# The last layer's x rows are stored while tokens are chosen, and the experts' weighed results are added onto them in the output

## The reference

```
def expert_choice_moe(h, w_router, w_gate, w_up, w_down):
    aff = softmax(h @ w_router)                        # 16 experts
    g, idx = lax.top_k(swapaxes(aff, 1, 2), cap)       # each expert takes its cap = 128 best tokens
    xs = h[idx]
    hid = silu(xs @ w_gate[e]) * (xs @ w_up[e])        # 1024 -> 512
    y = (hid @ w_down[e]) * g[..., None]               # 512 -> 1024
    return zeros((n, d)).at[idx.reshape(-1)].add(y.reshape(-1, d))

for l in range(2):
    ...
    x = x + g2 * expert_choice_moe(modulate_2(x, sh2, sc2), w_router[l], w_gate[l], w_up[l], w_down[l])
return x
```

## Time and profile before

| | us |
|---|---|
| median of 3 runs | 4846.79 (4844.91 to 4851.37) |
| span of the profiled execution | 4847.7 |
| choosing, from the first row copy to the experts' first instruction | 4444.9 to 4483.3 |
| experts of the last layer, to the start of the last stage | 4483.3 to 4821.2 |
| last stage, `add_store` | 4821.2 to 4847.7 |

### The profile page before, as it was taken

How to read it: one execution, slowest core, us unless ns; L and a number is a source line. 1 busy time by engine, 2 the same in 40 slices (tenths; PEclk the granted TensorE clock), 3 DMA queues, 4 the chain that set the end, 5 groups by cost and what they waited for, 6 DMA issues and landing times. The chain is left out here.

```text
span 4847.7 us, 89240 instructions
## 1 busy us (share of the span) xinstructions
PE 4373.6 (90%) x39266; PEld 3433.8 (71%) x39266; DVE 2090.7 (43%) x3010; ACT 1367.4 (28%) x2034; POOL 1059.3 (22%) x756
## 2 busy tenths in 40 slices
PE   6998996999998989999989889997999788996997
PEld 3878885999894468888867657764776574774775
DVE  2027545444444233323422244426665414434886
ACT  2114213222221110000012133324665212322774
POOL 2310123444432123333322010021221211010211
PEclk9999997999999999999999899998999888998998
DMA  7310100000007311111131000037997210002998
GB/s 279 100 49 7 49 23 27 4 4 4 4 4 293 109 35 49 51 48 48 48 108 32 29 20 1 18 126 276 304 301 235 84 33 23 1 27 109 345 375 287
DMA packets 322593, 480.30 MB, mean 99 GB/s; under 512 B 43665, under 2 KB 201322, under 8 KB 313042
## 3 DMA queue, kind: packets, MB, share of 16 engines
q1 hardware_dynamic: 301778, 399.61, 24.0%
q0 software_dynamic: 17024, 63.11, 4.6%
q10 hardware_dynamic: 3456, 12.58, 0.7%
HBM read 420.71 MB, written 54.53 MB: 98 GB/s over the span
## 5 line engine op out<-in xcount | busy, mean ns | idle before, releaser
L3919 DVE TENSOR_TENSOR l_experts_lo<-l_raw_room,l_experts_hi 128x1024 fp32r<-128x1024 f32 x256 | 300.0, 1219 | 59.0 <-ACT l_experts_hi L3852 58.5
L3852 ACT ACTIVATE l_experts_hi<-l_raw_room 128x1024 fp32r<-128x1024 f32 x256 | 256.0, 1058 | 63.8 <-PEq L3458 28.6
L185 PE MATMUL mlp_ps<-h_hi,mlp_w_hi 128*128 128x512 f32 x512 | 200.8, 392 | 9.1 <-DVE h_lo L595 9.1
L185 PE MATMUL mlp_ps<-h_lo,mlp_w_hi 128*128 128x512 f32 x512 | 199.9, 391 | 0.0
L185 PE MATMUL mlp_ps<-h_hi,mlp_w_lo 128*128 128x512 f32 x512 | 199.9, 390 | 0.0
L1812 POOL TENSOR_TENSOR rec_lv<-rec_ab,rec_masks 128x512 f32<-128x512 f32 x120 | 145.2, 1227 | 246.2 <-DVE rec_ab L1729 159.4
L1748 DVE TENSOR_TENSOR rec_x<-rec_x,rec_all_ps 128x1024 f32<-128x1024 f32 (+1 forms) x100 | 111.4, 1114 | 196.8 <-PE rec_all_ps L1530 196.8
L2393 ACT ACTIVATE mlp_hid_hi<-mlp_pos 128x1024 f32 x32 | 34.0, 1062 | 569.3 <-DVE mlp_pos L2403 569.3
L160 POOL CAST mlp_w_hi<-mlp_w 128x1024 fp32r<-128x1024 f32 x64 | 66.8, 1043 | 497.2 <-issue 228.0
L185 PE MATMUL mlp_ps<-mlp_hid_hi,mlp_w_hi 128*128 128x512 f32 x448 | 174.3, 389 | 0.0
L185 PE MATMUL mlp_ps<-mlp_hid_lo,mlp_w_hi 128*128 128x512 f32 x448 | 174.3, 389 | 0.0
(11 more groups left out here) (717 smaller groups left out, 11457.8 us busy)
## 6 DMA issues: line engine op xcount, KB each, us to landing
l_raw_room<-in_w_gate_dram SPq DMA_DIRECT2D x128, 512.0 KB, 6.7
l_raw_room<-in_w_up_dram SPq DMA_DIRECT2D x128, 512.0 KB, 8.0
l_experts_raw_down<-in_w_down_dram SPq DMA_DIRECT2D x64, 1024.0 KB, 8.8
rec_out_w_ada<-in_w_ada_dram SPq DMA_DIRECT2D x24, 1024.0 KB, 12.1
mlp_w<-in_w_mlp_up_dram SPq DMA_DIRECT2D x32, 512.0 KB, 3.9
mlp_w<-in_w_mlp_down_dram SPq DMA_DIRECT2D x32, 512.0 KB, 3.8
l_choose_w_ada<-in_w_ada_dram POOLq DMA_DIRECT2D x16, 1024.0 KB, 16.5
l_in_w<-in_w_in_dram SPq DMA_DIRECT2D x18, 512.0 KB, 3.9
```

Of the source, the lines that this page charges most:

```text
L185: mm = self.nc.tensor.matmul(ps[0:rows, c, 0:n], w[b][:, k, 0:rows], x[:, k, t0:t0 + n], start=(k + j == 0), stop=(k == kt - 1 and j == 2))
L3852: nc.scalar.activation(hi[:, q % RING], piece(e, u), ACT.Copy).then_inc(hi_done, 1)
L3919: nc.vector.tensor_tensor(lo[:, q % RING], piece(e, u), hi[:, q % RING].bitcast(F32), ALU.subtract).then_inc(lo_done, 1)
```

## The change

The last layer alone is changed; the layer before it keeps `acc_dram`, the zeroing and ACT's `outputs`. In the last layer:

- `choose_tokens` turns, copies and stores 16 row tiles instead of 8: after `hT`'s 8 to `h_dram` come x's 8 from `xT` to the output, through the same two buffers. PE then spreads the gate into `pT`, and ACT copies it to `gate_row`. Nothing is zeroed, and `acc_dram` isn't written.
- `run_experts` has DVE weigh `pY` by `gain` and `gate_row` in one instruction of 128x1024 (`gated_outputs`), between the low parts of the units 3 and 4, and ACT's `outputs` isn't called. POOL's indirect adds go to the output.
- `add_store` is gone.

```diff
-def add_store(nc, name, ident, xT, acc, gate, out):
...
@@ choose_tokens
+        jobs = [(hT, h_dram, t) for t in range(rows)]
+        if final is not None:
+            xT, x_dram, gate, gate_row = final
+            jobs += [(xT, x_dram, t) for t in range(rows)]
...
-                sp.wait_ge(zero_set, 1)
-                for t in range(rows):
-                    sp.dma_start(acc_dram[t * P:(t + 1) * P, :], zero[:]).then_inc(zero_stored, 16)
+                if final is None:
+                    sp.wait_ge(zero_set, 1)
+                    for t in range(rows):
+                        sp.dma_start(acc_dram[t * P:(t + 1) * P, :], zero[:]).then_inc(zero_stored, 16)
                 load_ahead(sp)
-                for t in range(rows):
-                    sp.wait_ge(row_copied, t + 1)
-                    sp.dma_start(h_dram[t * P:(t + 1) * P, :], out[:, t % 2]).then_inc(row_stored[t % 2], 16)
+                for i, (_, dram, t) in enumerate(jobs):
+                    sp.wait_ge(row_copied, i + 1)
+                    sp.dma_start(dram[t * P:(t + 1) * P, :], out[:, i % 2]).then_inc(row_stored[i % 2], 16)
...
-                        tr = nc.tensor.transpose(ps[:, t % 2, k], hT[:, k, t * P:(t + 1) * P], ident)
+                        tr = nc.tensor.transpose(ps[:, i % 2, k], src[:, k, t * P:(t + 1) * P], ident)
                     tr.then_inc(row_turned, 1)
...
+                if final is not None:
+                    pe.wait_ge(aff_copied, 1)
+                    for k in range(KT):
+                        mm = nc.tensor.matmul(pT[:, k * P:(k + 1) * P], gate[:, k:k + 1].to_broadcast([P, P]), ident,
+                                              start=True, stop=True)
+                    mm.then_inc(gate_spread, 1)
                 pe.wait_ge(chosen, 1)
...
+                if final is not None:
+                    act.wait_ge(gate_spread, 1)
+                    nc.scalar.activation(gate_row, pT[:, 0:D], ACT.Copy)
@@ run_experts
-                    if step >= 2:
+                    if step >= 2 and gate_row is None:
                         outputs(step - 2)
...
+                def gated_outputs(e):
+                    dve.wait_ge(used, place[e, UNITS - 1] + 1)
+                    if e >= 2:
+                        dve.wait_ge(added[e % 2], 16 * NG * (e // 2))
+                    nc.vector.scalar_tensor_tensor(ys[:, e % 2], pY[:].rearrange("p c t -> p (c t)"), gain[:, 0, e:e + 1],
+                                                   gate_row, ALU.mult, ALU.mult).then_inc(y_read, 1)
...
-                for step in range(E_N + 1):
+                for step in range(E_N + 2):
                     if step < E_N:
-                        for u in range(1 if step else 4, UP):
+                        for u in range(1 if step else 4, 4):
+                            low(step, u)
+                    if step >= 2 and gate_row is not None:
+                        gated_outputs(step - 2)
+                    if step < E_N:
+                        for u in range(4, UP):
                             low(step, u)
@@ second_layer
-                    scratch["acc"][0:tokens, :], raw, a["w_down_2"][layer])
+                    out if last else scratch["acc"][0:tokens, :], raw, a["w_down_2"][layer], gate_row)
```

More of the change, by code:

```diff
@@ L3413, in choose_tokens @@
 def choose_tokens(nc, name, ones, ident, norm_groups, w_router, groups, idx, gain, quarter_idx, h_dram, acc_dram,
-                  load_ahead, beside=None):
+                  load_ahead, beside=None, final=None):
     hT = norm_groups[0][3]
@@ L3438, in choose_tokens @@
         first, ahead = s.sb("first", [P, E_N]), s.sb("ahead", [P, E_N])
-        out, zero = s.sb("out", [P, 2, D]), s.sb("zero", [P, D])
+        out, zero = s.sb("out", [P, 2, D]), s.sb("zero", [P, D]) if final is None else None
+        jobs = [(hT, h_dram, t) for t in range(rows)]
+        if final is not None:
+            xT, x_dram, gate, gate_row = final
+            jobs += [(xT, x_dram, t) for t in range(rows)]
         pl = s.ps("pl", [P, 512])
@@ L3445, in choose_tokens @@
         zero_set, zero_stored = s.sem("zero_set"), s.sem("zero_stored")
+        gate_spread = s.sem("gate_spread")
         side = None if beside is None else beside(s, [pT[:, b * 512:(b + 1) * 512] for b in range(3)])
@@ L3504, in _ @@
                 tr.then_inc(turned, 1)
-                for t in range(rows):
-                    if t >= 2:
-                        pe.wait_ge(row_copied, t - 1)
+                for i, (src, _, t) in enumerate(jobs):
+                    if i >= 2:
+                        pe.wait_ge(row_copied, i - 1)
                     for k in range(KT):
-                        tr = nc.tensor.transpose(ps[:, t % 2, k], hT[:, k, t * P:(t + 1) * P], ident)
+                        tr = nc.tensor.transpose(ps[:, i % 2, k], src[:, k, t * P:(t + 1) * P], ident)
                     tr.then_inc(row_turned, 1)
@@ L3539, in _ @@
                     side.silu(act)
-                for t in range(rows):
-                    act.wait_ge(row_turned, t + 1)
-                    if t >= 2:
-                        act.wait_ge(row_stored[t % 2], 16 * (t // 2))
-                    nc.scalar.activation(out[:, t % 2], ps[:, t % 2].rearrange("p k t -> p (k t)"), ACT.Copy
+                for i in range(len(jobs)):
+                    act.wait_ge(row_turned, i + 1)
+                    if i >= 2:
+                        act.wait_ge(row_stored[i % 2], 16 * (i // 2))
+                    nc.scalar.activation(out[:, i % 2], ps[:, i % 2].rearrange("p k t -> p (k t)"), ACT.Copy
                                          ).then_inc(row_copied, 1)
+                if final is not None:
+                    act.wait_ge(gate_spread, 1)
+                    nc.scalar.activation(gate_row, pT[:, 0:D], ACT.Copy)
             @block.vector
@@ L3640, in load_first, with run_experts @@
             self.load(sp, 0, c)
-def run_experts(nc, name, ident, groups, idx, gain, quarter_idx, h_dram, acc_dram, raw_up, w_down):
+def run_experts(nc, name, ident, groups, idx, gain, quarter_idx, h_dram, acc_dram, raw_up, w_down, gate_row=None):
     caps = [g[2] for g in groups]
@@ L3973, in _, with second_layer @@
                             x_low(step + 1, g)
-def second_layer(nc, cst, ident, ones, a, scratch, layer, before, mod, next_mod, xT, cT):
+def second_layer(nc, cst, ident, ones, a, scratch, layer, before, mod, next_mod, xT, cT, out):
     last = next_mod is None
@@ L4031, in second_layer @@
         quarter_idx = None if last else sb(moe, "quarter_idx", [P, E_N], U32)
+        gate_row = sb(moe, "gate_row", [P, D])[:] if last else None
         with ExitStack() as tmp:
@@ L4038, in second_layer @@
                               nc, args[0], ident, (a["c_2"][0], a["c_ctx_2"]), a["w_ada_2"][layer + 1],
-                              a["b_ada_2"][layer + 1], next_mod, *args[1:], part=(1, 3)))
+                              a["b_ada_2"][layer + 1], next_mod, *args[1:], part=(1, 3)),
+                          (xT, out, col(mod, 5), gate_row) if last else None)
         run_experts(nc, nm + "experts", ident, groups, idx, gain, quarter_idx, scratch["h"][0:tokens, :],
-                    scratch["acc"][0:tokens, :], raw, a["w_down_2"][layer])
+                    out if last else scratch["acc"][0:tokens, :], raw, a["w_down_2"][layer], gate_row)
 def build(nc, a, cst, out):
@@ L4067, in build @@
             second_layer(nc, cst, ident[:], ones[:], a, scratch, layer, None if layer == 0 else mods[layer - 1],
-                         mods[layer], (mods + [None])[layer + 1], xT, cT)
-        add_store(nc, "out", ident[:], xT, scratch["acc"], col(mods[1], 5), out)
+                         mods[layer], (mods + [None])[layer + 1], xT, cT, out)
 def constants():
```

8 lines of the change are left out of this document (5 added, 3 removed).

## The result

The changed kernel takes 4822.01 us (median of 4 runs, 4810.57 to 4827.38) beside 4845.85 for the kernel before (4 runs, 4843.69 to 4851.37): a ratio of 0.9948, 95% interval 0.9935 to 0.9962, and 23.8 us less. The forecast was 4820, 26.7 us less.

The account below looks back on a forecast made before the run. DMA was taken to set the experts' pace, with an uncovered last stage all on the path. 26.5 - 0.8 + 1.0 = 26.7 us less, from 4846.8 to 4820.1, rounded to 4820; range 4813 to 4833.

Parts of the forecast that it names:

- The last stage goes: Program's end: the closing load, product, sum and store stage disappears, 26.5 us less 0.8 for the ending, 25.7 us less.
- x rows: Last choosing: eight more row tiles, 17.4 us at 2.17 a row, hide beside DVE's choosing; nothing, at most 1.9 us.
- Weighing on DVE: Experts' steps: one 1.283 us DVE instruction replaces ACT's two; nothing, since DMA sets the pace, at most 18 us.
- DVE becomes the bound: Rival in the experts' steps: the weighing costs 4 us partly exposed, 18 wholly, 4824 to 4838 in all; chance 0.12.
- The experts' end: Last expert: ACT's rounded copies start at once, first load landing after 4.9 us, PE starts earlier; 1.0 us less.
- The clock did not hold: Experts' end, rival: PE, idle for 2.65 us, might stay at the whole clock; 4817, within the forecast, not counted on.
- the bound's 2.7: Experts' end: upper bound on extra gain if PE's clock stays whole, seven pairs x (0.85 - 0.46) = 2.7 us.
- Adds into the output: Experts' adds to another place in memory: no cost taken; rival that they are slower, 4870 at 3.1 us each, chance 0.02.
- The total: Whole kernel: 26.7 us less than before, from a median of 4846.8 to 4820.1, rounded to 4820.

Follow-up runs that it names:

- e_rows_only: The kernel before, with the eight x rows also turned, copied and stored to the output in its last choosing; choosing 38.41 us, ratio to before 0.9998.
- e_rows_twice: The changed kernel with the x rows stored twice over, 24 rows in the last choosing; choosing 51.00 us, ratio to before 0.9968.
- e_weigh_twice: The changed kernel with DVE's weighing instruction issued twice per expert, first into a spare buffer; 333.2 us from first rounded copy to last add, ratio to before 0.9957.
- e_act_weighs: The changed kernel with ACT weighing in two instructions as before, the product with the gate left out; ratio to before 0.9940.
- e_after_third: The changed kernel run a third time, unedited; from last silu to last add's issue 17.95 us, ratio to before 0.9951.
- e_adds_to_acc: The changed kernel with the experts' adds going to the scratch accumulator, the output holding the x rows alone; ratio to before 0.9951.
- e_last_room: The changed kernel with the last expert's two down pieces loaded into the room its first two up pieces leave; end 17.85 us, ratio to before 0.9939.

## Why the prediction was right

**The last stage goes (25.7 us): right.** From the last add's issue to the end 35.9 us before and 10.5 now, 25.4 less; eleven other profiles with that ending have 10.3 to 10.9. The 0.3 us lie in the program's end: 4.5 us after the landing, where I had 4.0, and a landing of 6.0, not 6.2.

**x rows (nothing): right**, by the mechanism named: they lie beside DVE's choosing. `e_rows_only` shows the zero, `e_rows_twice` that it is the cover that makes it. The estimate of 17.4 us was high for this run (14.8), and its 2.17 us a row is near what eight more took (2.2).

**Weighing on DVE (nothing in the steps): right in the sum, not in each step.** The price, 1.280 us, and DVE's share, 92%, came as said. But the term treated all steps alike. In the early steps, where loads do not yet set the pace, the four low parts come later and the silu waits: 0.45 us for three steps. The rival "DVE becomes the bound" is thus true of those, and its 4 us were too high; over all steps the cost is 0.7 us by means of three profiles. `e_weigh_twice` shows how near the rest is: one instruction more, and DVE with its wait takes 19.4 us a step, as long as the later steps last anyway. The Trainium skill, "VectorE: DVE Perf Modes", section Specifications, has ScalarE closer to PSUM. No price of that shows in the runs: with ACT reading PSUM, the stretch to the last add takes 326.1 us (`e_act_weighs`), with DVE 325.0 to 326.8.

The term also left POOL out. Its issue of an add took 1.55 to 1.83 us in all but two of the 16 before. In the changed kernel five of 16 take 7.4, and land 14.6 to 16.7 us after their issue, not 9. The add of expert 13:

```profile
4789.95 7.44 POOL L3679 DMA_INDIRECT out_dram<-l_experts_ys,l_idx  x1 [10.79 <-DVE l_experts_ys L3902]
```

Behind that weighing DVE goes through six low parts without a pause, from 4789.07 to 4795.97. In `e_weigh_twice`, where DVE pauses once a step, for 0.8 us, 14 of 16 adds take 7.4; with the weighing late none takes over 2.9. That DVE's work holds POOL up is argued from this, not shown apart. No weighing waits for these adds.

**The experts' end (1.0 us): near in size (1.6 by three profiles), but in part by luck.** One pair of traces gave 2.6, which I took for the effect until `e_act_weighs` denied it. The step that was off is the load's landing. With the 4.9 us taken, PE's wait was to fall from 3.65 to 2.65. In the changed kernel's three profiles the load landed after 6.6, 7.6 and 4.9 us, and PE waited 3.08, 4.11 and 2.60: only 0.4 less in the mean. Where the landing was as taken, in `e_after_third` and `e_rows_twice` (5.0), the wait was as forecast, 2.60 in both. With `e_adds_to_acc` (7.7) five profiles have this end. In them the load is late where the add of expert 13 is (10.4 to 16.9 us to its landing, against 7.4 and 8.0); that this is the cause is not shown.

Most of the rest of the 1.6 has a source that the term doesn't name. With ACT's weighing PE also waited ahead of the last down products of expert 14, 0.87 to 1.05 us in three profiles; before:

```profile
4794.71 0.73 PE L3800 MATMUL l_experts_pY<-l_experts_hi,l_experts_h_hi 128*128 128x512 f32 x2 [0.91 <-DVE l_experts_lo L3919]
```

Their load landed 1.6 to 2.0 us after the last silu there. In the five profiles it landed 0.6 to 1.3 us ahead of it, and that wait is gone. Before's own end is also long by its clock: 0.51 from 4800.2 to 4807.1, 6.9 us, where `e_rows_only` and `e_act_weighs` have half the clock for some 3.4.

The clock did not hold in the profiled run. What it is worth, a pair of profiles tells. In `e_after_third` and `e_rows_twice` PE waits the same 2.60 us and goes on 8.5 us after the last silu, and the two loads land alike (4.9 and 4.8 us, 5.0 and 5.0). The first then has these rows, the second stays at 1.00 (last section):

```profile
4800.77 0.70 PE L3750 MATMUL l_experts_pY<-l_experts_hi,l_experts_h_hi 128*128 128x512 f32 x2 [2.60 <-DVE l_experts_lo L3869]
...
4802.23 1.05 PE L3750 MATMUL l_experts_pY<-l_experts_hi,l_experts_h_hi 128*128 128x512 f32 x2
```

Its granted clock is 0.50 from 4802.2 to 4805.6, and its end takes 17.95 us, not 16.49. So the clock was worth 1.5 us in this pair, not the bound's 2.7.

**Adds into the output: no difference**, as said; `e_adds_to_acc` shows it.

**The total.** Beside the kernel before of their own group, the medians of the changed kernel's three groups are 23.8, 23.1 and 23.2 us lower. Pooled over all groups, its 15 runs have a median of 4821.3 and the 55 of before 4847.5: 26.1 us less. The forecast's 26.7 lies just above all of these.

## What to carry to other kernels

A closing stage that only loads, adds and stores is worth its whole length if its parts can go under stages that wait for one engine; what they may take is read from the longest wait of the queue they join. An instruction added to an engine that is not the bound can still lengthen a step by standing ahead of what the next engine waits for. Placing it behind that brought the early steps back here, though not the total. Before a microsecond at the end of a program is explained, profile the same kernel a second time.

## What the hardware showed that I had not expected

An idle stretch of one length can end at either clock. In `e_last_room` PE waited 2.60 us ahead of the last expert's down products and went on at half the clock, 1.19 us for the first pair (row above), 1.06 for the next. In `e_rows_twice` it waited 2.60 us at the same place and stayed at the whole:

```profile
4813.55 0.70 PE L3750 MATMUL l_experts_pY<-l_experts_hi,l_experts_h_hi 128*128 128x512 f32 x2 [2.60 <-DVE l_experts_lo L3869]
4814.09 0.62 PE L3750 MATMUL l_experts_pY<-l_experts_lo,l_experts_h_hi 128*128 128x512 f32 x2
```

In the changed kernel it even went on at the whole clock after 3.08 us (0.70 for the first pair) and fell to half with the third pair (1.06); in `e_after_third` it went on at the whole after 2.60 us and fell with the fourth (1.05). What decides is not settled here. And executions differ in when they reach the same instruction, with the same instructions ahead of it: by 17.8 us over the 14 profiles, by 9.8 over the three of the changed kernel, whose time from there on differs by 1.4.
